# Second attention: the statistics' broadcast moved into the value unit, two logits moved ahead of the values' transposes

## What is computed

```python
def second_block(x, ...):
    hn = rms_norm(h, norm1_g[i])
    proj = hn @ w_in[i]
    a_b, a_c, a_h, q, k, v, c_u, c_v = jnp.split(proj, split_idx, axis=-1)
    ...
    q = rms_norm(q.reshape(bsz, s_len, ATTN_HEADS, HEAD_DIM), q_norm_g[i])
    k = rms_norm(k.reshape(bsz, s_len, ATTN_HEADS, HEAD_DIM), k_norm_g[i])
    v = v.reshape(bsz, s_len, ATTN_HEADS, HEAD_DIM)
    y_b = stick_breaking_attention(q, k, v).reshape(bsz, s_len, ATTN_W)
    ...

def stick_breaking_attention(q, k, v):   # for each block of 128 queries:
    z = jnp.einsum('bqhd,bkhd->bhqk', qi, kj) * scale
    causal = s_pos < t_pos
    log_beta = jax.nn.log_sigmoid(z)
    log_rem = jnp.where(causal, jax.nn.log_sigmoid(-z), 0.0)
    suffix = lax.cumsum(log_rem, axis=3, reverse=True) - log_rem
    weights = jnp.where(causal, jnp.exp(log_beta + suffix), 0.0)
    o = jnp.einsum('bhqk,bkhd->bqhd', weights, vj)
```

## Time and profile before

| | |
|---|---|
| median of 3 runs | 3144.33 us (3144.18 to 3148.64) |
| the profiled execution | 3144.82 us, span 3142.7 us |
| mean granted clock | 0.973 |
| PE busy | 2970.7 us (95%) |
| DVE busy | 1594.9 us (51%) |
| POOL busy | 1019.7 us (32%) |
| ACT busy | 683.7 us (22%) |

### The profile page before, as it was taken

One profiled execution on the slowest core, in us unless ns is written; L12 is line 12 of the kernel. 1 busy time (PEld: TensorE's weight loads), 2 busy tenths in 40 slices (PEclk: granted clock), 3 DMA queues, 4 the chain that ended last, 5 costly groups with the idle time before them and its releaser, 6 DMA issues. The chain is left out here.

```text
span 3142.7 us, 37444 instructions
## 1 busy us (share of the span) xinstructions
PE 2970.7 (95%) x14666; PEld 2433.4 (77%) x14666; DVE 1594.9 (51%) x1731; ACT 683.7 (22%) x984; POOL 1019.7 (32%) x467
## 2 busy tenths in 40 slices
PE   6898999996999999999999899999999999999999
PEld 5787788885878888888787666668778888888787
DVE  6666566666555326515547456563543233242445
ACT  4444422222211000000132244441210000000131
POOL 2111122220334434444343211113334444344443
PEclk8999999997999999999999899999999999999999
DMA  3001010100211111111111200011211111111112
GB/s 115 24 24 31 27 33 28 34 27 16 85 41 50 50 47 47 47 47 52 52 50 47 88 21 20 15 34 34 94 47 47 47 42 50 49 47 53 51 50 81
DMA packets 42442, 144.91 MB, mean 46 GB/s; under 512 B 5600, under 2 KB 6368, under 8 KB 42080
## 3 DMA queue, kind: packets, MB, share of 16 engines
q1 hardware_dynamic: 36576, 123.06, 12.1%
q10 hardware_dynamic: 5760, 20.38, 1.7%
HBM read 132.05 MB, written 8.49 MB: 45 GB/s over the span
## 5 line engine op out<-in xcount | busy, mean ns | idle before, releaser
L516 POOL TENSOR_TENSOR w_hi<-w_raw,der 128x1024 fp32r<-128x1024 f32 (+1 forms) x228 | 420.4, 1844 | 2074.9 <-PE ps L562 2045.3
L560 PE MATMUL ps<-a_hi,w_hi 128*128 128x512 f32 x2336 | 947.8, 406 | 28.7 <-DVE a_lo L1442 9.9
L562 PE MATMUL ps<-a_hi,w_lo 128*128 128x512 f32 x2336 | 922.0, 395 | 0.0
L561 PE MATMUL ps<-a_lo,w_hi 128*128 128x512 f32 x2336 | 921.1, 394 | 0.0
L519 POOL TENSOR_TENSOR w_lo<-w_raw,w_hi 128x1024 fp32r<-128x1024 f32 (+1 forms) x230 | 595.4, 2589 | 24.1 <-ACT w_hi L1648 6.2
L560 PEld LDWEIGHTS ps<-a_hi,w_hi 128*128 128x128 f32 x2336 | 447.2, 191 | 122.1 <-issue 16.7
L562 PEld LDWEIGHTS ps<-a_hi,w_lo 128*128 128x128 f32 x2336 | 445.1, 191 | 96.1
L561 PEld LDWEIGHTS ps<-a_lo,w_hi 128*128 128x128 f32 x2336 | 447.1, 191 | 84.1
L560 PE MATMUL ps<-b_hi,w_hi 128*128 128x512 f32 x1120 | 439.6, 392 | 32.6 <-DVE b_lo L1413 15.3
L561 PE MATMUL ps<-b_lo,w_hi 128*128 128x512 f32 x1120 | 437.7, 391 | 0.0
L562 PE MATMUL ps<-b_hi,w_lo 128*128 128x512 f32 x1120 | 437.4, 391 | 0.0
(11 more groups left out here) (263 smaller groups left out, 2984.6 us busy)
## 6 DMA issues: line engine op xcount, KB each, us to landing
w_raw<-in_w_mix SPq DMA_DIRECT2D x54, 512.0 KB, 3.4
w_raw<-in_w_gu SPq DMA_DIRECT2D x44, 512.0 KB, 3.4
w_raw<-in_w_f SPq DMA_DIRECT2D x40, 512.0 KB, 3.4
w_raw<-in_w_f SPq DMA_DIRECT2D x32, 384.0 KB, 3.0
w_raw<-in_w_ple SPq DMA_DIRECT2D x20, 512.0 KB, 3.4
w_raw<-in_w_out SPq DMA_DIRECT2D x16, 512.0 KB, 3.4
w_raw<-in_w_dn SPq DMA_DIRECT2D x16, 512.0 KB, 3.4
x<-in_x SPq DMA_DIRECT2D x8, 512.0 KB, 8.4
```

The costliest lines, as they stand in the source:

```text
L516: nc.gpsimd.tensor_tensor(w_hi[:, s, 0:cols[s]], w_raw[:, s, 0:cols[s]], zero.to_broadcast([P, cols[s]]), ALU.add).then_inc(w_hi_done, 1)
L560: mm(ps[:, bank, :], wh, hi[:, k, cols], start=(k == 0), stop=False)
L561: mm(ps[:, bank, :], wh, lo[:, k, cols], start=False, stop=False)
L562: last = mm(ps[:, bank, :], wl, hi[:, k, cols], start=False, stop=(k == nk - 1))
```

## The change

On PE the second half of the value unit is cut behind its third k-step: three k-steps, both broadcasts, five k-steps. Behind the unit, the wait for qk2_ready comes first, then the logits of segment 0 and of segment 1, and only then the wait for sv's second half and the transposes of sv. The wait for sv_ready moves into turn 1 of the loop, ahead of the first turn of weights. On ACT the copy of svt moves behind the first two sigmoids sb of the head. The parameter `free` of `k_step` is new and no call uses it.

```diff
-            def gemm_half(u, hf, s, hi, lo, nk, wait_k=None):
-                for k in range(nk):
+                return last
+
+            def gemm_half(u, hf, s, hi, lo, nk, wait_k=None, first=0, end=None):
+                for k in range(first, nk if end is None else end):
...
                 st_sums(c_buf, blk2, 2, 0, True)
                 st_sums(ss, blk2, 2, 16)
-                gemm_half(u + 2, 1, (u + 2) % 2, a_hi, a_lo, KT)
+                gemm_half(u + 2, 1, (u + 2) % 2, a_hi, a_lo, KT, end=3)
                 st_bcast(N_QK + p, 2, 4, 0, True)
                 st_bcast(N_QK + p, 2, 2, 16)
-                pe.wait_ge(acc_free, half_no(u + 2, 1))
-                transposes(sv, 6, sv_tr)
+                gemm_half(u + 2, 1, (u + 2) % 2, a_hi, a_lo, KT, first=3)
                 pe.wait_ge(qk2_ready, 2 * p + 2)
                 slots = filling(*sb_fill(p), 2 * NSEG + 2)
                 logits(p, 0)
-                pe.wait_ge(sv_ready, p + 1)
+                logits(p, 1)
+                pe.wait_ge(acc_free, half_no(u + 2, 1))
+                transposes(sv, 6, sv_tr)
                 for n in range(NSEG + 2):
-                    if n + 1 < NSEG:
+                    if 2 <= n + 1 < NSEG:
                         logits(p, n + 1)
+                    if n == 1:
+                        pe.wait_ge(sv_ready, p + 1)
...
                 st_sqrt(N_QK + p, 32)
-                act.wait_ge(sv_tr, p + 1)
-                av(svt[:, :, :], banks(6).rearrange("p (c e) -> p c e", c=KT), ACT.Copy).then_inc(sv_ready, 1)
                 act.wait_ge(x_out, 16 * KT)
                 for n in range(NSEG + 2):
                     if n < NSEG:
                         betas(p, n, 0, True)
                         betas(p, n, 1, True)
+                    if n == 0:
+                        act.wait_ge(sv_tr, p + 1)
+                        av(svt[:, :, :], banks(6).rearrange("p (c e) -> p c e", c=KT),
+                           ACT.Copy).then_inc(sv_ready, 1)
```

More of the change, by code:

```diff
@@ L547, in _, with k_step @@
             mm = nc.tensor.matmul
-            def k_step(u, hf, k, s, hi, lo, nk, bank=None):
+            def k_step(u, hf, k, s, hi, lo, nk, bank=None, free=None):
                 bank = hf if bank is None else bank
@@ L554, in k_step @@
                     pe.wait_ge(w_split, u + 1)
-                if k == 0 and bank == hf and not (isinstance(u, int) and half_no(u, hf) <= 2):
+                if k == 0 and free is not None:
+                    pe.wait_ge(acc_free, free)
+                elif k == 0 and bank == hf and not (isinstance(u, int) and half_no(u, hf) <= 2):
                     pe.wait_ge(acc_free, half_no(u, hf) - 2)
```

## The result

The changed kernel takes 3119.06 us (median, 3117.72 to 3120.33) where the kernel before takes 3145.38 on the same chip: a ratio of 0.9915 (0.9897 to 0.9932), 0.85% less. The prediction was 3124.0 with a range of 3118 to 3133. The profiled execution took 3117.72 with a span of 3115.6, 27.1 less than before.

The account below looks back on a forecast made before the run. PE bounds the kernel, so only its idle or slow-clock time can go. T0 to turn falls from 15.02 (last head 15.51) to 3.84 + 6.1 = 9.94, 20.8 us in all: 3144.8 - 20.8 = 3124.0, range 3118 to 3133.

Parts of the forecast that it names:

- The broadcast's insertion, 3.84: On PE, 64 broadcast matmuls inside the value unit's second half make its last matmul come 3.84 us later.
- The low stretch behind the sums, costed at 0 with 0.5 a head: PE's low clock after the sums: broadcast moves in, product matmuls out; taken as 0, 0.5 us a head either way.
- The wait for sv and the low clock behind it: Behind the value unit, PE's idle 3.18 us before the transposes goes, and the clock of 0.56 after it becomes 1.00.
- DVE's scans blocked by POOL, turn at T1 + 6.1: POOL's weight split holds DVE's first scans; first turn of weights at T1 + 6.1, PE waiting 0.8, last head 0.1.
- T1: Predicted start of the value unit's last matmul on PE, 3.84 us later than before the change.
- 6.6 as a bound: Worse blocking case: both first DVE scans stand behind POOL's w_lo, first turn at T1 + 6.6; +2.0 us in all.
- The sum: Attention gain of 5.08 us in three heads and 5.57 in the last, 20.8 in all, giving 3124.0; own range 3119.5 to 3129.
- The segment loops, costed at nothing: Steps behind the first turn stay PE's; DVE some 0.7 us later costs nothing, or 2.8 if its cover is gone.
- POOL does not block the scans: Rival, chance 0.13: DVE's first scans run unhindered, the turn comes with PE, gain 23.3 us, time 3121.5.
- The clock falls again: Rival, chance 0.14: half rate from the transposes on, turn 3.1 us later; 3130.2 in two heads, 3136.4 in four.
- DVE's own shift only: Rival, chance 0.08: DVE binds the segment loop, so only its shift of 2.9 us a head counts, 11.6 in all: 3133.2.
- The low clock outlasts the broadcast: Slower case, chance 0.03: half rate behind the sums lasts through broadcast to turn, 6.1 us more a head: 3169.

Follow-up runs that it names:

- sums apart: Changed kernel with the sums' 32 thin matmuls parted into 16 for queries and 16 for keys, two k-steps between: 3115.22 us, run again 3118.63.
- short split: Changed kernel with POOL's two splits behind each head's value unit working on 128 of 1024 columns: 3118.15 us, ratio 0.9915.
- broadcast alone: Changed kernel with the old order behind the value unit: transposes of sv before logits 0, svt copied before the sigmoids: 3126.97 us, ratio 0.9942.
- the seven profiles named above: Kernel before, changed kernel twice, broadcast alone, short split, logits moved without the broadcast, broadcast after six k-steps: medians from 3118.15 to 3145.38 us.

## Why the prediction was right

- **The broadcast's insertion, 3.84.** Heads 0 and 3 had one low stretch behind the sums before and after: 10.44 to 14.27 and 10.43 to 14.27, 3.83 and 3.84.
- **The low stretch behind the sums, costed at 0 with 0.5 a head.** This term was mis-sized. A head has no, one or two stretches of 3.4 us there, at 1.6 each. Head 1 went from one to none and head 2 from two to one: 3.2 us that the sum didn't have. How many a run draws is in part luck: the changed kernel had three and then two. In part it may be the change: with the broadcast behind the unit 8 heads had 12 of them, with it inside 20 heads had 16, and no run shows why. That they follow the sums' block is shown by the kernel with the sums apart.
- **The wait for sv and the low clock behind it.** Both gone; logits 0 wait for nothing. The two multiplications ended at 1789.72, 1.1 ahead of the logits (1.3 predicted).
- **DVE's scans blocked by POOL, turn at T1 + 6.1.** Measured 6.03, and the run with the short split shows that the cause is POOL. But the scans did not lie as laid out, and the close agreement is in part luck. I had one scan slip in between w_hi and w_lo. In the trace sb was ready only after w_hi had ended, w_lo started at T1 + 2.44, and the first scan at T1 + 2.56 stood behind it until T1 + 5.11. That is the case that I had set at 6.6 as a bound; it comes out at 6.03 because w_lo ended at T1 + 4.83 and not at 5.05, with nothing pushing it back, and two scans, mask and product of 1.1 in all followed. PE alone is faster than I took it (4.77 and 5.12, not 5.3 and 6.0), because the eight matmuls of the two logits step in 0.85 and not 1.4, and in the last head the transposes and the third logits in 0.85 each. So PE waits 1.2 and 0.85, not 0.8 and 0.1. That error moves no time, since PE isn't what ends last there.
- **The sum.** With equal clock a head gains 15.02 - 3.84 - 6.03 = 5.15 (5.08 predicted), the last 5.63 (5.57). Three and one are 21.1; head 1 had 0.26 less to give, and 3.2 of clock make 24.05 against 20.8. With the 3.04 that differ ahead of the attention, the profiled executions differ by 27.1. So with equal clock the sum is right to 0.1 us, and the 5 us by which the median lies under 3124.0 are low stretches, for which the prediction had allowed 2.0, and the part ahead, for which it had allowed nothing. The sum's own upper bound is added wrong: 3124.0 + 2.0 + 2.8 + 2.0 is 3130.8 and not 3129; the range of 3118 to 3133 holds it.
- **The segment loops, costed at nothing.** 57.47 to 57.45 and 86.41 to 86.39.
- **The rivals.** "POOL does not block the scans" is out: 2.86 where 0.74 is usual. "The clock falls again" is out for this kernel, but near: with the broadcast alone it happened in head 0. No run shows a fall through transposes alone; the eight here ran with the clock at 1.00. "DVE's own shift only" is out: it gave 11.6 us where the heads gave 24.05 (20.8 with equal clock). "The low clock outlasts the broadcast" is out: in head 0 the low stretch reached 1 us into it and the clock came back under thin matmuls, at 1784.0; the broadcast took 4.06 from start to start and not 3.64, outside the 3.6 to 3.8 that the prediction gave as a sign.

## What to carry to other kernels

Where PE waits for a vector engine, look at what stands between the wait and its cause on both engines: moving work of PE in front of the wait pays twice if the clock was falling behind it. Before an operation that PE needs is put behind others, ask whether a third engine can hold those others: an eviction standing behind a mask and a product cost 18.7 us of the attention by two places in a list. And judge an edit of a few microseconds by the stretch that it touches; the total carries the clock's stretches of everywhere else.

## What the runs showed of the hardware

- Thin matmuls can let the clock fall though PE counts as busy all the time: behind 32 matmuls onto two columns in a row (3.5 us) it fell in 5 of 8 heads of the changed kernel and in 23 of 28 heads of the seven profiles named above; behind 16 and 16 with one k-step between in 2 of 4 heads, with two k-steps between in none of 16. The idle time of 2.57 brought a low stretch too, in 4 of 4 heads; waits of 0.8 and 0.7 close together brought one in 1 of 4.
- A low stretch of 3.4 us costs 1.6 to 1.7. The time behind the attention, the same code in all, came out near 1001.1, 1002.8, 1004.3, 1010.8 and 1012.2, which are near 0, 1, 2, 6 and 7 times 1.6 above the least. The clock's own records have, against the changed kernel, six low stretches more there at 1010.8 and eight at 1012.2, so one costs 1.4 to 1.6 there.
- POOL's split holds small operations of DVE for as long as its own operation lasts: a mask of 0.27 took 1.98 (w_hi 1.96), a product of 0.29 took 2.38, and a scan of 0.4 took 2.55 (w_lo 2.39). An eviction out of PSUM beside a w_hi took its usual 0.68.
